# Dense gates of the second sample tile by scatter-add DMAs into a zeroed DRAM tensor, head by head, in place of one-hot products

## The reference, cut to what matters

```python
q = (x @ w_q).reshape(N, PEER_HEADS, 2, PK_DIM // 2)
s = einsum("nhcd,ckd->nhck", q, sub_keys)
s1, i1 = top_k(s[:, :, 0], 16)
s2, i2 = top_k(s[:, :, 1], 16)
cand_s = s1[..., :, None] + s2[..., None, :]
cand_i = i1[..., :, None] * N_KEYS + i2[..., None, :]
top_s, pos = top_k(cand_s, 16)
idx = take_along_axis(cand_i, pos)
gate = softmax(top_s)
act = gelu(einsum("thkd,td->thk", u_tab[idx], x)) * gate
out = einsum("thk,thkd->td", act, v_tab[idx])
```

## Time and profile before

| | |
|---|---|
| median of 3 runs | 2677.42 us |
| profiled execution | 2680.38 us, span 2678.6 us |
| TensorE busy | 2604.6 us, 97% of the span |
| VectorE busy | 1658.9 us, 62% |
| ScalarE busy | 1022.3 us, 38% |
| GpSimd busy | 720.7 us, 27% |
| moved by DMA | 708.88 MB, mean 265 GB/s |
| granted TensorE clock, mean | 0.987 of full speed |

### The profile page before, as it was taken

The page is one execution under the profiler, slowest core; times in us unless marked ns, Lnnn a source line. Parts: engine busy times, 40 slices in busy tenths (PEclk is TensorE's granted clock), DMA queues, the critical chain, the costliest instruction groups (busy, mean ns, idle before and its releaser), DMA issues. The chain is left out here.

```text
span 2678.6 us, 39466 instructions
## 1 busy us (share of the span) xinstructions
PE 2604.6 (97%) x15833; PEld 2307.6 (86%) x15833; DVE 1658.9 (62%) x3306; ACT 1022.3 (38%) x1531; POOL 720.7 (27%) x688
## 2 busy tenths in 40 slices
PE   7998999999999999999999889999999999999998
PEld 6997789999999997777779679999999999777775
DVE  3447687879344456555576569987934445655556
ACT  3444433345433333333352554334543333333333
POOL 1001020000111117777723003000011111777773
PEclk9998899999999999999999989999999999999999
DMA  9653486547798869999964124344779886999995
GB/s 307 219 170 139 148 300 215 165 189 287 262 360 317 315 217 388 391 383 382 386 254 127 64 97 137 119 147 188 287 266 365 313 312 217 391 389 390 393 385 202
DMA packets 233941, 708.88 MB, mean 265 GB/s; under 512 B 22432, under 2 KB 154912, under 8 KB 211488
## 3 DMA queue, kind: packets, MB, share of 16 engines
q1 hardware_dynamic: 172912, 516.86, 52.7%
q0 software_dynamic: 60032, 189.01, 19.2%
q10 hardware_dynamic: 816, 0.48, 0.1%
HBM read 602.31 MB, written 103.98 MB: 264 GB/s over the span
## 5 line engine op out<-in xcount | busy, mean ns | idle before, releaser
L1410 PE MATMUL hidden_ps<-h_hi,u_hi 128*128 128x384 f32 x2016 | 680.3, 337 | 4.1 <-issue 3.1
L1410 PE MATMUL hidden_ps<-h_hi,u_lo 128*128 128x384 f32 x2016 | 674.0, 334 | 0.0
L1410 PE MATMUL hidden_ps<-h_lo,u_hi 128*128 128x384 f32 x2016 | 674.0, 334 | 0.0
L2300 DVE TENSOR_TENSOR v_lo<-v_slot,v_hi 128x1024 fp32r<-128x1024 f32 x248 | 303.9, 1225 | 269.2 <-ACT v_hi L2164 269.2
L2164 ACT ACTIVATE v_hi<-v_slot 128x1024 fp32r<-128x1024 f32 x248 | 263.0, 1060 | 515.0 <-PE out_ps L2093 503.0
L2093 PE MATMUL out_ps<-v_hi,act_hi 128*128 128x512 f32 x992 | 389.7, 393 | 0.0
L2093 PE MATMUL out_ps<-v_lo,act_hi 128*128 128x512 f32 x992 | 386.3, 389 | 0.0
L2093 PE MATMUL out_ps<-v_hi,act_lo 128*128 128x512 f32 x992 | 385.9, 389 | 0.0
L1410 PEld LDWEIGHTS hidden_ps<-h_hi,u_hi 128*128 128x128 f32 x2016 | 378.6, 188 | 6.9 <-issue 6.8
L1410 PEld LDWEIGHTS hidden_ps<-h_lo,u_hi 128*128 128x128 f32 x2016 | 378.7, 188 | 0.0
L1410 PEld LDWEIGHTS hidden_ps<-h_hi,u_lo 128*128 128x128 f32 x2016 | 378.5, 188 | 0.0
(11 more groups left out here) (502 smaller groups left out, 3968.9 us busy)
## 6 DMA issues: line engine op xcount, KB each, us to landing
u_slot<-in_peer_u SPq DMA_DIRECT2D x64, 2048.0 KB, 9.1
v_slot<-in_peer_v SPq DMA_DIRECT2D x64, 2048.0 KB, 9.9
hidden<-hidden_ring SPq DMA_DIRECT2D x64, 768.0 KB, 5.8
spread_gates<-spread SPq DMA_DIRECT2D x16, 2048.0 KB, 7.2
hidden_in<-hidden SPq DMA_DIRECT2D x64, 512.0 KB
ada_w_ring<-in_ada_w SPq DMA_DIRECT2D x48, 512.0 KB, 6.1
even_w_ring<-in_even_w SPq DMA_DIRECT2D x16, 1024.0 KB, 7.5
ada_w_ring<-in_ada_w SPq DMA_DIRECT2D x16, 1024.0 KB, 6.1
```

The lines of the kernel that those rows point to most:

```text
L1410: mm = pe.matmul(PH_[:, b, 0:T], u[:, b, k * P:(k + 1) * P], x[:, k, :], start=(k == 0 and part == 0), stop=(k == KB - 1 and part == 2))
L2300: dve.tensor_tensor(lo, V[o // JC % 2][:, o % JC, :], hi.bitcast(F32), ALU.subtract).then_inc(vl, 1)
```

## The change

The table of gates is split in two. The first sample tile (tile 1) is made as before, now in 8 rounds of 16 tokens into a `WD` of 4 groups (8 MB). The second (tile 2, `ADDED`) goes into a DRAM tensor of its own for each layer, `WADD[l]` (8 MB), which is filled with zeros from SBUF by one DMA earlier in the layer (in `mlstm` for layer 0, in `attend` for layer 1). VectorE now numbers tile 2 first, works out for each token and pick the place in the table (`added_numbers`), and GpSimd adds the gates with 128 indirect DMAs of 128 elements each: 16 for a head, then a wait until all 16 have landed, then the next head. TensorE transposes only two tiles, tile 1 and then tile 0. `TAIL_N` is (15, 4, 4), `GATE_N` 8, every round has two hidden products, and `LAST_N` is 9. In `peer_front` SyncE waits for all additions before it loads the second half of `W0` and spills the last hidden values. Every later read of the table is two DMAs of half the size.

```diff
+        GROUPS_1 = P // TG
+        WD = nc.dram_tensor("spread_gates", [P, GROUPS_1, N_KEYS, TG], F32).ap()
+        WADD = [nc.dram_tensor(f"added_gates{l}", [P, GROUPS_1, N_KEYS, TG], F32).ap() for l in range(DEPTH)]
+        def zero_gates(sp, l, zeros, done):
+            n = zeros.shape[-1]
+            to = WADD[l].rearrange("p g j t -> p (g j t)").rearrange("p (a n) -> p a n", n=n)
+            sp.dma_start(to, zeros.unsqueeze(1).broadcast_to([P, GROUPS_1 * N_KEYS * TG // n, n])).then_inc(done, 16)
...
-        TAIL_N, GATE_N, LAST_N = (11, 4, 4, 4), TD // 16, 6
-        IN_TURN = [2 if h % 6 == 2 else 1 for h in range(GATE_N)]
+        TAIL_N, GATE_N, LAST_N = (15, 4, 4), P // 16, 9
+        IN_TURN = [2] * GATE_N
+        ADDED, TURNED = 2, (1, 0)
...
-                    sp.wait_ge(w_done, TD // 4)
-                    sp.dma_start(W0, WD[:, :, EARLY:EARLY + JC, :].rearrange("p g j t -> p g (j t)")).then_inc(w0_in, 16)
+                    sp.wait_ge(w_done, P // 4)
+                    sp.dma_start(W0[:, 0:GROUPS_1], WD[:, :, EARLY:EARLY + JC, :].rearrange("p g j t -> p g (j t)")).then_inc(w0_in, 16)
+                    sp.wait_ge(added, 16 * PH * TOPK)
+                    sp.dma_start(W0[:, GROUPS_1:], WADD[l][:, :, EARLY:EARLY + JC, :].rearrange("p g j t -> p g (j t)")).then_inc(w0_in, 16)
                     spill(EARLY // 4 - 1)
...
                     gate_to_rows(pool, l, 5, GROW[2 * l + 1], gate_stored, gate_landed)
                     pool.wait_ge(gate_landed, 16)
+                    table = WADD[l].rearrange("p g j t -> (p g j t)").unsqueeze(1)
+                    pool.wait_ge(to_add, 1)
+                    for h in range(PH):
+                        for k in range(TOPK * h, TOPK * (h + 1)):
+                            pool.indirect_dma_start(table, bass.IndirectOffsetOnAxis(ap=IDXA[:, k:k + 1], axis=0), GADD[:, k:k + 1], None,
+                                                    compute_op=ALU.add).then_inc(added, 16)
+                        pool.wait_ge(added, 16 * TOPK * (h + 1))
...
+                    def added_numbers():
+                        token = CST[:, C_IDX:C_IDX + 1]
+                        first, second = GS[:, ADDED, 1, :], GS[:, ADDED, 2, :]
+                        v.seq(dve.tensor_copy(TOKU[:, :], token))
+                        v.seq(dve.tensor_single_scalar(TOKU[:, :], TOKU[:, :], 5, ALU.logical_shift_right))
+                        v.mark(dve.scalar_tensor_tensor(TOKF[:, :], TOKU[:, :], float(N_KEYS * TG - TG), token, ALU.mult, ALU.add))
+                        v.mark(dve.scalar_tensor_tensor(first, first, float(GROUPS_1 * N_KEYS), second, ALU.mult, ALU.add))
+                        v.mark(dve.tensor_copy(GADD[:, :], GS[:, ADDED, 0, :]))
+                        v.wait()
+                        dve.tensor_scalar(IDXA[:, :], first, float(TG), TOKF[:, :], ALU.mult, ALU.add).then_inc(to_add, 1)
...
-                    for t in range(TT):
+                    for t in (ADDED, *TURNED):
...
+                            if t == ADDED and c == 1:
+                                added_numbers()
...
-                        sp.dma_start(W[m % 2], WD[:, :, j:j + JC, :].rearrange("p g j t -> p g (j t)")).then_inc(w_in[m % 2], 16)
+                        for n, gates in enumerate((WD, WADD[l])):
+                            sp.dma_start(W[m % 2][:, n * GROUPS_1:(n + 1) * GROUPS_1], gates[:, :, j:j + JC, :].rearrange("p g j t -> p g (j t)")).then_inc(w_in[m % 2], 16)
...
                     load_ahead(sp, ahead)
+                    sp.wait_ge(zero_made, 1)
+                    zero_gates(sp, 0, ZERO[:, :], zero_out)
...
                     sp.wait_ge(out_st, 48)
+                    sp.wait_ge(zero_out, 16)
```

More of the change, by code:

```diff
@@ L1453, in peer_front @@
                 WS = M.at("spread", M.phase + 36864, [P, 2, P, TG])
-                I1, I2, G1, G2 = (M.at(n, M.picks + 1024 * i, [P, TD, 2], F16) for i, n in enumerate(
+                I1, I2, G1, G2 = (M.at(n, M.picks + 1024 * i, [P, P, 2], F16) for i, n in enumerate(
                     ("first_at", "second_at", "gate_hi", "gate_lo")))
-                GD, GR = M.at("gate_twice", M.v0, [P, TD, 2]), M.at("gate_rest", M.v0 + 3072, [P, P, 2])
+                GD, GR = M.at("gate_twice", M.v0, [P, P, 2]), M.at("gate_rest", M.v0 + 3072, [P, P, 2])
                 IOB = M.at("iota_b", M.phase + 69632, [P, P], F16)
+                GADD, IDXA = M.at("added_gate", M.picks + 512, [P, P]), M.at("added_at", M.picks + 1536, [P, P], U32)
+                TOKU, TOKF = M.at("token_u", M.picks + 2560, [P, 1], U32), M.at("token_f", M.picks + 3584, [P, 1])
+                to_add, added = sem(st, "gates_to_add"), sem(st, "gates_added")
                 (qh, ql, q_done, q_taken, s_done, s_taken, s_used, v_step, e_in, e_out, picked, turned, pk_taken, lr_ready,
@@ L1528, in _ @@
                             sp.dma_start(LN[:, 1, :], spread(I["ln_b"][l, 0:1, :], D)).then_inc(ln_in, 16)
-                        for g in range(TD // TG):
+                        for g in range(GROUPS_1):
                             if n == gates_at + sum(IN_TURN[:2 * g + 2]) - 1:
@@ L1599, in hidden, with picks @@
                         hidden_products(pe, PH_, UH, UL, HH, HL, n, uh, ul, g_done, h_done)
[L1601 to L1604, removed]
+                    def picks(n):
+                        t = TURNED[n]
+                        pe.wait_ge(picked, n + 2)
+                        if n:
+                            pe.wait_ge(pk_taken, n)
                         for kind in range(3):
@@ L1819, in key_numbers @@
                     def key_numbers(t, c):
-                        if t == 0 and c == 0:
+                        if t == ADDED and c == 0:
                             dve.wait_ge(x_back, TT)
@@ L2226, in early_load @@
                         pool.dma_start(HV[:, e % 2], HD[:, e, :, P:T]).then_inc(early_in[e % 2], 16)
-                        pool.dma_start(WE[:, e % 2], WD[:, :, JC * e:JC * e + JC, :].rearrange("p g j t -> p g (j t)")).then_inc(early_w[e % 2], 16)
+                        for n, gates in enumerate((WD, WADD[l])):
+                            pool.dma_start(WE[:, e % 2, n * GROUPS_1:(n + 1) * GROUPS_1],
+                                           gates[:, :, JC * e:JC * e + JC, :].rearrange("p g j t -> p g (j t)")).then_inc(early_w[e % 2], 16)
                     pool.memset(SDW, 0.0).then_inc(zeroed, 1)
@@ L2622, in _ @@
                     load_ahead(sp, ahead)
+                    sp.wait_ge(zero_made, 1)
+                    zero_gates(sp, 1, ZERO[:, :], zero_out)
+                    sp.wait_ge(zero_out, 16)
+                @block.gpsimd
+                def _(pool):
+                    pool.memset(ZERO[:, :], 0.0).then_inc(zero_made, 1)
+                    pool.wait_ge(zero_made, 1)
                 @block.tensor
```

37 lines of the change are left out of this document (22 added, 15 removed).

## The result

The changed kernel takes 2867.57 us (median of 4 runs, 2867.01 to 2868.5), the kernel before 2677.62 us beside it (4 runs, 2674.08 to 2680.5): ratio 1.0714, 95% interval 1.0701 to 1.0728, 190 us slower. The forecast was 2702 us with 2655 to 2815 as its range. The sign was right, the size was not: the loss is nearly eight times the forecast's.

The account below looks back on a forecast made before the run. TensorE was taken as the bound, with GpSimd's additions ending peer_front late: 2 x (8.5 meeting + 2.5 clock + 0.5 spill) + 1.5 zeroing = +24.5 on 2680.38, 2704.9, given as 2702 us for a median; range 2655 to 2815.

Parts of the forecast that it names:

- So 0.95 + 0.30: GpSimd in peer_front: each addition holds it 0.95 us like a gather, plus a 0.30 us issue gap.
- a gather costs the same 0.95 whatever it moves: Argument against dearer additions: a gather holds GpSimd 0.95 us, and gathers of whole rows run beside those of 128 elements.
- Rival 2: An addition costs GpSimd or DMA more than a gather: 2809 us at 1.4 us each, 2924 at 1.88; chance 0.25.
- X: GpSimd's time for one head in peer_front, 16 additions and the wait for their landing: forecast 25.0 us.
- The reading of the long gathers: Gathers take 1.16 us instead of 0.95 when a VectorE CAST falls into one; peer_front has few casts in this stretch.
- The landing: From a head's last addition's issue to its landing in peer_front: 6.1 us, 5.65 plus 0.45 for the reading before adding.
- TensorE's saving: In peer_front, eight one-hot rounds (15.2 us) and one tile's transposes (0.73 us) go: 15.9 us a layer.
- the end of its front at 705.8: Without any new wait, TensorE would end layer 0's peer_front at about 705.8 us instead of 721.7.
- the room of 22.1 us a head: GpSimd's time for each of 8 heads in peer_front before TensorE would notice: 176.8 us in all.
- the formula: Change in total time is 16 X - 375.5 us, as long as GpSimd is last to the meeting ending peer_front.
- rival 1: The additions keep up in peer_front and TensorE's saving is kept: 2647 us if nothing waits; chance 0.18.
- Zeroing: Filling the 8.4 MB tables with zeros: nothing in attend, +1.5 us at the mLSTM block's end.

Follow-up runs that it names:

- experiment 3: The changed kernel with each addition replaced by an indexed write of the gates to the same places, without adding: 2715.83 us (one run).
- experiment 2: The changed kernel with each addition replaced by a gather of 128 elements from the same places: 2719.04 us (one run).
- experiment 4: The changed kernel with the same 128 additions a layer, each on 64 partitions instead of 128: 2848.43 us (one run).
- experiment 6: The changed kernel with VectorE's low parts in the front as SCALAR_TENSOR_TENSOR instead of TENSOR_TENSOR: 2874.23 us (one run).
- experiment 1: The changed kernel without the 128 additions a layer and SyncE's wait for them: 2648.23 us, ratio 0.9905 to the kernel before.
- experiment 5: The changed kernel with a quarter of the sample tokens added instead of half, 64 full additions a layer: 2660.17 us, ratio 0.9949 to the kernel before.

## Why the prediction was wrong

**The step that failed is "So 0.95 + 0.30"**, the price of an addition taken from the gathers. The additions in the groups of instructions of after (busy, mean ns of one, idle before them):

```profile
L1563 POOL DMA_INDIRECT added_gates<-added_gate,added_at x256 | 433.9, 1695 | 316.5 <-DVE added_at L1909 184.5 <-issue 91.2 <-DMA added_gates<-added_gate,added_at 40.7
```

A head is 16 holds of 1.695, 15 gaps of 0.38 (91.2 / 240) and a pause of 2.9: 27.1 + 5.7 + 2.9 = 35.7, and 36.0 by the chain. The forecast in the same terms: 16 x 0.95 + 15 x 0.30 + (6.1 + 0.1 - 0.95) = 15.2 + 4.5 + 5.25 = 25.0. The holds are 11.9 us a head too short. Of these 16 x 0.59 = 9.4 are the addition as such (1.558 against 0.968 in experiment 3), the rest mostly VectorE.

**The rule behind it, "a gather costs the same 0.95 whatever it moves", held for gathers (0.947 us in experiment 2, 0.946 in the median for whole rows of `peer_v` in the kernel before) and told nothing of additions.** Rival 2 named the right place, the hold of an addition on GpSimd. Its reason, that each element is read, added and written, is not what experiment 4 shows: of 1.558 us the 128 elements account for some 0.3. Its figures, 1.4 us for 2809 and 1.88 for 2924, enclose the result. I gave it 0.25 and ended the range inside it, at X = 32; the measured X is 36.0. The row of 1.88 us was the upper bound that I had named; the range should have gone up to it.

**The reading of the long gathers was wrong as well.** I put the 1.16 us of the gather at 997.33 down to the CAST. The TENSOR_TENSOR that starts at 996.45 ends at 997.68, 0.35 us after that gather began; less 0.14, as in experiment 6, this is the 0.21 by which it is longer than 0.95. The gather at 996.08 was ahead of it. With that reading I should have expected lengthened additions all through the front, which is full of such operations. In experiment 2 it is 0.21 us for each gather (1.162 in the mean against 0.947), 3.4 us a head:

```profile
L1563 POOL DMA_INDIRECT added_gate<-added_gates,added_at x256 | 297.4, 1162 | 307.6 <-DVE added_at L1909 184.9 <-issue 79.1 <-DMA added_gate<-added_gates,added_at 43.6
```

**The landing was too dear in the mean.** I took 6.1 us from the issue, of which 0.45 stood for a reading that no run shows by itself; with gathers it was 1.16 + 3.1 (43.6 us in 14 pauses), with additions 1.7 + 2.9. Where the DMA engines are busy the landing of additions took longer than that (pauses of 5.8 to 6.8 behind the hold), but four of the first layer's seven pauses lie where they are not. For gathers, by luck, this error and the one on VectorE cancel in part: gathers in the additions' place give X of about 26.6, and 16 X - 375.5 = +50 against the measured +42.

**Right, by their own steps:** TensorE's saving (30.3 us with the zeroing; the kernel without additions is 28.3 us faster than the one before), the end of its front at 705.8 (704.3), GpSimd's start at 529.0 (527.06), the room of 22.1 us a head, the formula (X = 36.0 gives +200, measured +190) and rival 1's time without a wait (2647; 2648.2 in experiment 1). Zeroing was forecast at +1.5: TensorE's wait at the mLSTM block's end is 3.7 us in the kernel before and 5.7 after, but it lies between 4.1 and 8.5 in the runs with the same 8 MB of zeros, and is 3.7 with 4 MB (experiment 5).

## What to carry to other kernels

A chain of DMAs that one engine issues is priced by how long each holds that engine, and a form of DMA that no row shows must be given the whole width between the rows until it has run once by itself; a range should reach the upper bound that its own rows give. When the price turns out to be per instruction, ask how few full ones the slack has room for: half as many made a loss of 190 us a gain of 16. And before idle time in front of a meeting is filled, look at what then has less time behind it: here VectorE's wait for the gates loaded again and the lower clock took back all that had been gained.

## What the runs showed that was not expected

- An indirect DMA that adds 128 elements to DRAM holds GpSimd 1.56 us, one that writes them 0.97, one that reads them 0.95; in packets it is 144 against 32.
- An indirect DMA that begins inside a VectorE operation on two SBUF tensors is longer by what is left of that operation, less 0.12 to 0.14 us (43 of 128 additions, by 0.44 us in the mean); one that began before it is not.
- A small store queued behind the 8 MB of zeros kept SyncE's queue for 30.55 us, where it took 0.38 in the kernel before:

```profile
219.86 0.58 SPq L135 DMA_DIRECT2D added_gates<-zeros  x1
220.49 30.55 SPq L2912 DMA_DIRECT2D out_new_m<-m_rows  x1
...
252.20 1.09 SPq L2915 DMA_DIRECT2D out_new_mlstm<-prompt_mstate  x1
```

With 4 MB of zeros (experiment 5) the same row has 19.39 us. What it waits for is not shown.
